# Hybrid decoder layer on one core: first projections between the last x tiles, first weight tile earlier in the load queue

## The reference, cut to what matters

```python
h = concat([meta (16 tokens), x (1024 tokens)])           # (1040, 1024), float32
u = rmsnorm(h, norm_w)
proj = u @ w_in                                           # w_in: (1024, 4104)
hg_q, hg_f, hg_i, hg_z, gd_qkv, gd_z, gd_a, gd_b = split(proj)
# HGRN2, 4 heads: gated linear attention in chunks, gated rmsnorm
# Gated DeltaNet, 4 heads: causal conv of width 4 + silu on q, k, v; g and beta from gd_a, gd_b
#   (8 columns of w_in: the gate); triangular solve per chunk; gated rmsnorm
h = h + concat(y_hg, y_gd) @ w_out
out = rmsnorm(h, final_norm_w)[16:]
```

## Time and profile before

| what | us |
|---|---|
| time, median of 3 runs (784.63 to 786.99) | 785.84 |
| the profiled execution | 786.99 |
| span in its profile | 785.3 |
| TensorE matmul busy | 725.2 (92% of the span) |
| TensorE weight loads busy (beside matmuls) | 688.1 |
| VectorE busy | 450.0 |
| GpSimd busy | 343.1 |
| ScalarE busy | 305.3 |
| the front: last matmul starts | 88.38 |
| first matmul of the next block | 90.22 |

### The profile page before, as it was taken

How to read it: one execution, slowest core, us unless ns; L and a number is a source line. 1 busy time by engine, 2 the same in 40 slices (tenths; PEclk the granted TensorE clock), 3 DMA queues, 4 the chain that set the end, 5 groups by cost and what they waited for, 6 DMA issues and landing times. The chain is left out here.

```text
span 785.3 us, 13610 instructions
## 1 busy us (share of the span) xinstructions
PE 725.2 (92%) x4852; PEld 688.1 (88%) x4852; DVE 450.0 (57%) x1011; ACT 305.3 (39%) x782; POOL 343.1 (44%) x449
## 2 busy tenths in 40 slices
PE   7799999999999999899999999999999859999975
PEld 7599999989998999899999999999899848888764
DVE  6645354378882552888824528987244266765255
ACT  6435422624543235335442263354422332132133
POOL 5573342166552421665533216754333056654124
PEclk9899999999999999999999999999999968999998
DMA  8246225030213263805355403022243042211015
GB/s 252 23 55 85 28 32 86 19 51 5 41 42 51 35 80 24 51 6 36 49 34 65 77 11 55 1 42 56 39 115 83 3 156 97 94 48 48 1 34 207
DMA packets 77030, 45.52 MB, mean 58 GB/s; under 512 B 30894, under 2 KB 72212, under 8 KB 76964
## 3 DMA queue, kind: packets, MB, share of 16 engines
q1 hardware_dynamic: 76964, 44.66, 32.4%
HBM read 36.41 MB, written 8.24 MB: 57 GB/s over the span
## 5 line engine op out<-in xcount | busy, mean ns | idle before, releaser
L221 PE MATMUL proj<-uTh,w_high 128*128 128x352 f32 (+1 forms) x768 | 262.1, 341 | 4.8 <-PEq L168 4.8
L221 PE MATMUL proj<-uTh,w_low 128*128 128x352 f32 (+1 forms) x768 | 246.3, 321 | 0.0
L221 PE MATMUL proj<-uTl,w_high 128*128 128x352 f32 (+1 forms) x768 | 245.9, 320 | 0.0
L221 PEld LDWEIGHTS proj<-uTh,w_high 128*128 128x128 f32 x768 | 145.1, 189 | 5.8 <-issue 5.7
L221 PEld LDWEIGHTS proj<-uTl,w_high 128*128 128x128 f32 x768 | 145.0, 189 | 0.0
L221 PEld LDWEIGHTS proj<-uTh,w_low 128*128 128x128 f32 x768 | 144.3, 188 | 0.0
L239 POOL TENSOR_TENSOR w_low<-w_raw,w_high 128x256 fp32r<-128x256 f32 (+1 forms) x54 | 71.0, 1314 | 95.5 <-ACT w_high L231 40.7
L1508 PE MATMUL mix<-level_x 128*128 128x128 f32 x448 | 67.0, 284 | 9.8 <-issue 4.4
L1508 PEld LDWEIGHTS mix<-level_x 128*128 128x128 f32 x448 | 62.2, 197 | 14.6 <-issue 13.2
L1150 POOL TENSOR_TENSOR f_suffix<-f_suffix,f_prefix 128x192 f32<-128x192 f32 x84 | 56.2, 669 | 22.1 <-DVE f_prefix L1337 14.1
L1347 DVE COPY_PREDICATED hg_scores<-mask_st,mix 128x384 f32<-128x384 uint8 (+1 forms) x96 | 52.1, 542 | 18.7 <-PE mix L1508 18.1
(11 more groups left out here) (309 smaller groups left out, 1381.8 us busy)
## 6 DMA issues: line engine op xcount, KB each, us to landing
w_raw<-in_w_in SPq DMA_DIRECT2D x32, 512.0 KB, 8.3
x_tile<-in_x SPq DMA_DIRECT2D x8, 512.0 KB, 7.4
w_raw<-y_scratch SPq DMA_DIRECT2D x8, 384.0 KB, 4.5
decay<-gamma_scratch SPq DMA_DIRECT2D x4, 576.0 KB, 4.1
landing<-in_w_out SPq DMA_DIRECT2D x4, 512.0 KB, 7.6
landing<-in_x SPq DMA_DIRECT2D x3, 512.0 KB, 3.6
y_scratch<-gd_y SPq DMA_DIRECT2D x6, 192.0 KB, 1.8
decay<-in_w_out SPq DMA_DIRECT2D x2, 512.0 KB, 4.0
```

The source lines that it names most:

```text
L221: last = pe.matmul(acc[:, 0:tw], w[j % 2][:, k, :], u[:, k, t0:t0 + tw], start=(k == 0 and i == 0), stop=(k == KT - 1 and i == 2))
```

## The change

On PE the gate pieces move behind the transposes of all tiles. 3 parts of the projection are put behind tile 6, 3 behind tile 7 and 10 behind tile 8: together the first two pieces. Then come the three gate pieces, the third piece, and the small gate transposes; what follows them moves back by two pieces each. On SP weight tile 0 and the two parameter broadcasts stand ahead of x tile 5 instead of behind x tile 8. ACT rounds weight tile 0 behind tile 4, POOL makes its low part there. The diagonal matrices are made from the identity in SBUF; its copy in PSUM and the semaphore for it are gone. Two memsets and one select of POOL move behind its tile loop. The number of tiles that ACT and POOL work ahead goes from 4 to 3, with the step written ahead of the tile's own work instead of behind it.

```diff
-    ident_ps = bank[5][:, 384:384 + P]
-    AHEAD = 4
+    BESIDE = {6: range(0, 3), 7: range(3, 6), 8: range(6, 2 * PARTS)}
+    AHEAD = 3
...
@@ sync
-            for i in range(2, XS):
+            for i in range(2, 5):
+                load_x(i)
+            load_tile(0, tile_cols("gd", GD_KINDS[0], 0))
+            sp.dma_start(pr[:, 0, :], A_log[0:1, :].broadcast_to([P, HEADS])).then_inc(prm_in, 16)
+            sp.dma_start(pr[:, 1, :], dt_bias[0:1, :].broadcast_to([P, HEADS])).then_inc(prm_in, 16)
+            for i in range(5, XS):
                 load_x(i)
             sp.dma_start(gate_raw[:, :, :], w_in_v[:, :, AB_COLS:AB_COLS + 2 * HEADS]).then_inc(gate_in, 16)
             for i in range(XS, NC):
                 full(sp, front, ("x", i - XS, 1))
                 load_x(i)
-            load_tile(0, tile_cols("gd", GD_KINDS[0], 0))
-            sp.dma_start(pr[:, 0, :], ...)
-            sp.dma_start(pr[:, 1, :], ...)
@@ gpsimd
             for i in range(NC):
-                low_part(pool, 2 * i + 1)
                 if i + AHEAD < NC:
                     rstd_tile(i + AHEAD)
-            early_low(0)
+                low_part(pool, 2 * i + 1)
+                if i == 4:
+                    early_low(0)
@@ scalar
             for i in range(NC):
+                if i + AHEAD < NC:
+                    square_tile(i + AHEAD)
...
                 for half in range(2):
                     high_part(2 * i + half)
-                if i + AHEAD < NC:
-                    square_tile(i + AHEAD)
-                if i == 5:
+                if i == 4:
+                    early_high(0)
+                if i == 6:
                     act.wait_ge(gate_in, 16)
                     act.copy(gate_h, gate_raw[:, :, :]).then_inc(gate_high, 1)
+                    act.wait_ge(prm_in, 32)
+                    act.activation(ea[:, :], pr[:, 0, :], ACT.Exp).then_inc(gate_exp, 1)
-            early_high(0)
-            take_gate(0)
...
+            take_gd_front(act, 0, split=False)
             early_high(1)
-            take_gd_front(act, 0, split=False)
+            take_gd_front(act, 1, split=False)
+            for g in range(len(PIECES)):
+                take_gate(g)
+            take_gd_front(act, 2, split=False)
+            early_high(2)
+            first_tap(0)
@@ vector
-                dve.tensor_scalar(diag[i % DIAGS][0:w, 0:w], ident_ps[0:w, 0:w], rstd[0:w, i:i + 1], None,
+                dve.tensor_scalar(diag[i % DIAGS][0:w, 0:w], ident[0:w, 0:w], rstd[0:w, i:i + 1], None,
                                   ALU.mult).then_inc(scaled, 1)
...
-                if n == 13:
+                if n == 14:
                     dve.wait_ge(gate_high, 1)
...
+            conv_taps(1)
             for g in range(NG):
                 decay_diff(dve, 0, g, dec_in, dec_sub)
-            conv_taps(1)
@@ tensor
-            pe.transpose(ident_ps, ident[:, :], ident[:, :]).then_inc(ident_there, 1)
...
-                if i == 6:
-                    gate_piece(0)
-            gate_piece(1)
-            gate_piece(2)
-            project(range(0, PARTS))
+                project(BESIDE.get(i, ()))
+            for g, (t0, tw) in enumerate(PIECES):
+                ...                                   # the body of gate_piece(g)
+            project(range(2 * PARTS, 3 * PARTS))
             pe.wait_ge(gate_out, len(PIECES))
...
-            project(range(PARTS, 3 * PARTS))
+            project(range(3 * PARTS, 5 * PARTS))
```

More of the change, by code:

```diff
@@ L415, in _ @@
             pool.tensor_copy(mask_st[:, 0, :], ident[:, :]).then_inc(consts, 1)
[L416 to L421, removed]
             def early_low(n):
@@ L550, in _ @@
             act.activation(gw[:, 5, :, :], gw[:, 3, :, :], ACT.Ln, bias=1.0).then_inc(gate_exp, 1)
[L551 to L554, removed]
             take_gd_front(act, 3, split=False)
+            take_gd_front(act, 4, split=False)
             act.wait_ge(gate_step, 12)
@@ L633, in _ @@
             last.then_inc(mask_set, 1)
-            dve.wait_ge(ident_there, 1)
-            for i in range(DIAGS - 1):
+            dve.wait_ge(const0, 4)
+            for i in range(AHEAD - 1):
                 diag_tile(i)
@@ L644, in _ @@
             for n in range(2 * NC):
-                if n % 2 == 0 and n // 2 + DIAGS - 1 < NC:
-                    diag_tile(n // 2 + DIAGS - 1)
+                if n % 2 == 0 and n // 2 + AHEAD - 1 < NC:
+                    diag_tile(n // 2 + AHEAD - 1)
                 norm_part(n)
@@ L728, in project @@
                     project_part(pe, n, 1)
[L730 to L738, removed]
-                        last = pe.matmul(gbank[g % 2][0:4 * HEADS, 0:tw], gate_w[:, k, :], u[:, k, t0:t0 + tw],
-                                         start=(k == 0 and n == 0), stop=(k == KT - 1 and n == 1))
-                last.then_inc(gate_done, 1)
+            pe.wait_ge(rows_in, 80)
             pe.wait_ge(const0, 4)
-            pe.transpose(ident_ps, ident[:, :], ident[:, :]).then_inc(ident_there, 1)
-            pe.wait_ge(rows_in, 80)
             ap, done = take(pe, front, "rows")
@@ L757, in _ @@
                     last.then_inc(done, 1)
-                if i == 6:
-                    gate_piece(0)
-            gate_piece(1)
-            gate_piece(2)
-            project(range(0, PARTS))
+                project(BESIDE.get(i, ()))
+            for g, (t0, tw) in enumerate(PIECES):
+                for low in u_low:
+                    pe.wait_ge(low, 1 + -(-(t0 + tw - META) // P))
+                pe.wait_ge(gate_low, 1)
+                if g >= 2:
+                    pe.wait_ge(gate_out, g - 1)
+                for k in range(KT):
+                    for n, u in enumerate((uh, ul)):
+                        last = pe.matmul(gbank[g % 2][0:4 * HEADS, 0:tw], gate_w[:, k, :], u[:, k, t0:t0 + tw],
+                                         start=(k == 0 and n == 0), stop=(k == KT - 1 and n == 1))
+                last.then_inc(gate_done, 1)
+            project(range(2 * PARTS, 3 * PARTS))
             pe.wait_ge(gate_out, len(PIECES))
@@ L778, in _ @@
             pe.matmul(ap[:, 0:HEADS * NC], ones[:, :], g_all, start=True, stop=True).then_inc(done, 1)
-            project(range(3 * PARTS, 3 * PARTS + 3))
+            project(range(5 * PARTS, 5 * PARTS + 3))
             pe.wait_ge(gate_step, 10)
@@ L782, in _ @@
             pe.transpose(ap[0:HEADS * NC, 0:P], gam[:, :, :].rearrange("p h c -> p (h c)"), ident[:, :]).then_inc(done, 1)
-            project(range(3 * PARTS + 3, 4 * len(PIECES) * PARTS))
+            project(range(5 * PARTS + 3, 4 * len(PIECES) * PARTS))
     end_block()
```

14 lines of the change are left out of this document (6 added, 8 removed).

## The result

| kernel | median us | kernel before, same chip | ratio, 95% interval |
|---|---|---|---|
| changed | 790.81 (788.96 to 792.2, 6 runs) | 786.13 (782.72 to 787.77, 6 runs) | 1.0064 [1.0039, 1.0089] |
| changed, second series | 789.91 | 787.03 | 1.0023 [1.0007, 1.0039] |
| changed, third series | 790.74 | 787.19 | 1.0047 [1.003, 1.0064] |

The changed kernel is slower: by 5.0, 1.8 and 3.7 us, if each ratio is taken times 787. All three intervals lie above 1. I had forecast 786.1 with a range that ended at 789.9; the median is above it. The profiled execution took 788.67 us with a span of 786.9. The profiled execution of the second series was disturbed; its profile is not read and its time is left out.

What follows compares the result with a forecast made beforehand. PE, busy 92% of the span, was taken to bound the kernel. Restart +0.5 us, gap -0.3 and clock 0 summed to +0.2, giving 786.1 us against the median, with a range of 782.7 to 789.9.

Steps and rivals of the forecast that it cites:

- How the front adds up: Front's end is PE's restart after its last long pause, plus the dense work behind it, plus the clock loss.
- the gap of 0.29: PE's one idle gap after its restart, at 38.88; the gate pieces no longer meet it: -0.3 us.
- the clock's 2.2: Clock falls in PE's pause and stays at half speed 4.3 us after restart, losing 2.2 us, same as before: 0.
- The set of work behind the restart, and the new wait: PE has the same work left after its restart; its wait for the gate becomes one for weight tile 0's low part.
- The landing of tile 5: The weight tile ahead in the queue delays x tile 5 by 4.1 us, to 16.8, between 15.2 and 18.5.
- The chain from tile 5 to `w_low`: ACT and POOL work from tile 5's landing to the weight's low part takes 11.5 us, ending at 28.3.
- L: Time at which x tile 5 lands and its square can start; forecast 16.8, from 15.2 to 18.5.
- port: Rival: DVE's diagonals from SBUF wait for POOL's low parts; +1.3 us for one on the path, +2.4 for two; chance 0.15.
- warm: Rival: PE's clock does not fall in the pause or recovers sooner; -2.0 us, -3.6 with early landing; chance 0.24.
- held: The forecast case: PE's wait for the gate becomes a wait for w_low of like length; +0.2 us; chance 0.47.
- Long half speed: Rival: PE stays slow 9.2 us after its restart, not 4.3, losing another 2.4 us; +2.6 us; chance 0.14.
- The sum: Front's end: restart 28.3 instead of 27.76, +0.5; gap -0.3; clock 0; total +0.2 us, from -1.4 to +1.9.

Runs made afterwards that it cites:

- e2: The changed kernel with the diagonals made from the identity in PSUM again; 788.22 us, ratio 1.0020 to the kernel before.
- e7: The changed kernel with the two parameter broadcasts behind x tile 8 again, weight tile 0 still ahead of tile 5; 790.58 us, ratio 1.0047 to the kernel before.
- e9: The changed kernel itself, measured again as the third series; 790.74 us, ratio 1.0047 to the kernel before.
- e4: The changed kernel with SP's old load order and the identity in PSUM, PE's new order kept; 784.25 us, ratio 0.9964 to the kernel before.
- e3: The changed kernel with weight tile 0 and the two broadcasts behind x tile 8, as before; 785.5 us, ratio 0.9977 to the kernel before.
- e5: The kernel before with only the diagonals' identity taken from SBUF; 790.7 us, ratio 1.0047 to the kernel before.
- e6: The kernel before with only SP's order changed, weight tile 0 and both broadcasts ahead of x tile 5; 791.08 us, ratio 1.0061 to the kernel before.
- e8: e4 with projection piece 0 cut: high-part matmuls behind tile 6, low-part ones behind tile 7, second piece behind tile 8; 779.83 us, ratio 0.9921 to the kernel before.
- e10: The changed kernel with only projection piece 0 cut by operand, early weight tile and SBUF identity kept; 788.2 us, ratio 1.0012 to the kernel before.
- e1: The changed kernel itself, measured again as the second series; 789.91 us, ratio 1.0023 to the kernel before.

## Why the prediction was wrong, step by step

**How the front adds up: right, and better than I knew.** Take the front's end less the restart. The changed kernel has 58.47 us, e2 58.48, e7 58.47. Before it is 60.93; less the gap of 0.29 and the clock's 2.2 that is 58.4. e9 has 60.03, e4 59.75, e3 60.10; each of these showed a clock near one half at or soon after the restart. So the dense work is 58.4 to 58.5 us in all, and only two terms vary: the restart, and 0 to 1.6 us of clock. With PE's old order the same sum, less the gap of 0.3, leaves 3.0 us of clock in e5 and 1.8 in e6. The clock's share is a remainder, but it fits the rows: e9 did 16 matmuls where the first profile did 29, which is 1.7 us of full speed.

**The set of work behind the restart, and the new wait: right.** The wait for the gate became a wait for `w_low`, released by POOL, as said. It is 1.72 us and not 2.8, since a part of the stall had moved ahead of tile 5's transposes.

**The landing of tile 5: the step that failed.** I took the weight tile's service as 4.1 us, the middle of 2.5 and 5.6, and so 16.8 for the landing, 18.5 at most. Measured were 18.63, 19.08, 19.41 and more: against the 12.7 of the kernel before, the weight tile in front cost tile 5 5.9 us in the first profile, 6.4 and 6.7 in e9 and e2, and not 4.1. The lower bound should have had no weight: the 2.5 us between the landings of tile 8 and weight tile 0 were what was left over: the weight tile had been issued at 11.47, and part of it was served beside x tiles. The 5.6 us between two weight tiles was the price of one, and the row of GB/s in 17.60:23.00, 76 against 374, would have said so. I had read the DMA share, which is as high in both, as the measure of the queue. For the changed kernel's first profile the error is 1.8 us; with e9 and e2, 2.3 and 2.6 us.

**The chain from tile 5 to `w_low`: right in its parts, one port short.** I had L + 11.5. Without the port it is 11.05 (e2) and 11.90 (e4); with it 12.56, 12.54 (e9), 12.55 (e7) and 12.33 (e3). The rival "port", at 0.15, came true: the diagonals of tiles 5, 6 and 7 took 1.30 to 1.40 us. On the path that is 1.0 us against the forecast chain and 1.5 against e2, where tile 5 is late too; with tile 5 on time it is 0.4 (e3 against e4). Two diagonals had been priced at +2.4. Why only a part of their waits reaches the path is not tried. My argument against it was that POOL waits for ACT ahead of most low parts. It does. But ACT's second half releases POOL some 0.6 us after its first has released DVE's low part, which takes 0.69 us; so DVE comes to the diagonal as POOL starts, and in the changed kernel the two meet at each of these tiles. This is read from the rows, not tried by itself. The Trainium skill (SBUF - State Buffer, Who interferes with whom) has the rule that who comes second waits for the whole instruction; 0.28 against 1.21 and 1.22 us in e5, beside a low part of 1.27, agrees with it.

**The clock: right on what happens in a pause, wrong on where.** I had the loss as before, 2.2 us, and one pause. There were two, and it fell in the first. Its half speed then fell on the transposes of tiles 5 and 6, where PE had to wait anyway. At the restart the loss was 0 (the first profile, e2, e7) or 1.6 (e9). That is the rival "warm" in one execution and "held" in another of the same kernel. "Long half speed" did not come in the changed kernel; in e5 the half speed lasted somewhat longer than before, 5.7 us instead of 4.3. Its argument stays unexplained: the 43 matmuls in 5.40:15.00 came at a granted clock of 1.00, so the row doesn't show half speed.

**The sum, with what was measured.** Restart 31.19 - 27.76 = +3.43, gap -0.29, clock -2.2: +0.94, where +0.97 is seen. With e9: 31.62 - 27.76 = +3.86, -0.29, -0.6: +2.97, where +2.96 is seen. I had +0.5, -0.3 and 0. The restart is 2.9 us later than forecast, 1.8 of it the landing and 1.0 the ports. The landing is a mis-sized term; the ports were a rival that the sum left out. That the first profile's front still ends only 0.8 us behind the forecast 88.9 is luck: the clock's 2.2 us came back in just that execution. The range had slips too. Late L with long half speed is +1.9 + 2.4 = +4.3 and not +4.1, and warm with an early L is -3.6 and not -3.2, which gives 782.2 to 790.1; the median lies above that as well.

**What stays open.** The times of the changed kernel stand 1.8 to 5.0 us above the kernel before, the fronts of the two good profiles 1.0 and 3.0. With e2 to e8 and e10 the time follows the front within 0.4 us (e3, e4, e8, e10) to 1.8 us (e5). Where it is over half a microsecond, the surplus is on the slow side. It also decides the range: the fronts alone, +1.0 and +3.0 on 785.84, would have stayed inside it (786.8 and 788.8).

A profile is one execution, and not always a typical one: the first profile's, 788.67 us, is faster than all six timed ones of its series, and e9's, 793.84, is slower than all but one of its ten. What lies behind the front is the same code in all kernels, and yet it is not equally long. Span less front is 696.6 us before, 697.2 in the changed kernel's first profile, 700.4 in e9, 701.2 in e6 and 694.4 in e8. The starts of the blocks show where e9 lost against the first profile. The third block behind the front took 68.9 us before and in the first profile (248.33 to 317.26) and 71.4 in e9 (250.36 to 321.74). Its first 10 us, in e9 and then in the first profile:

```profile
250.36:260.36 10.00, 10.00 (x60) 9.92 (x61) 1.55 (x5) 4.67 (x19) 3.87 (x6) 0.83 0.49 72
248.33:258.33 10.00, 9.99 (x72) 9.92 (x73) 2.52 (x9) 5.12 (x19) 4.93 (x7) 1.00 0.50 72
```

The clock fell there in e9, and just so in e3 (60 matmuls at 0.83), which has the old load order. The fifth block took 69.0 us in the first profile, 69.6 before, 71.0 in e9 and 72.7 in e6; PE waits there for DVE (`gd_n`) for 1.78 us in e9 and 1.93 in e6, and not at all in the first profile. So a part of the surplus is clock and waits in unchanged code, which differ from one execution of a kernel to the next. Whether the change makes them more frequent, by where it leaves the later loads or in some other way, no run here tells, and so the rest of the medians' difference stays open.

**What the parts are worth.** By differences of ratios: PE's order -0.36% (e4), the cut of piece 0 another -0.43% (e8 less e4, on two chips), SP's order +0.46% (e1 to e3) or +0.61% (e6), the identity +0.13% (e3 to e4; their intervals overlap) or, in the kernel before, +0.47% (e5). These are differences of single measurements with intervals of 0.2 to 0.3% to each side, so those that lie close are not told apart.

## What to carry to other kernels

Before a load is moved ahead of others in a full queue, read the GB/s of the stretch in which it is served, not the busy share: the price of being in front goes by its size over its own rate, and who is behind it may be more urgent. Here 512 KB at 111 and 76 GB/s are 4.7 and 6.9 us, and tile 5 was 5.9 to 7.8 us late. When two engines are released by the same third one, their instructions start together; an operand that moves from PSUM to SBUF can then meet the other engine's instruction each time, and a scaling of 0.35 us takes 1.3. Where a matmul group waits for one of its operands only, start it with the parts that need the others: that gained 0.35 to 0.43% here, about as much as PE's new order (0.36%).

## What the hardware showed that I had not expected

- Weight tiles (512 KB) came at 76 to 111 GB/s, x tiles of the same size at 374, the DMA share being 0.94 to 1.05 in all three windows. In 5.40:15.00 the DMA view has 1087 of 1927 packets under 512 B and nearly all others over 2 KB before, and 942 of 1546 between 512 B and 2 KB in the changed kernel; it moved 2.11 MB instead of 3.36. Whether the packets' size is what makes the weight tile slow is not tried:

```profile
DMA packets 1546, 2.11 MB, mean 220 GB/s; under 512 B 207, under 2 KB 1149, under 8 KB 1546
```

- An x tile behind a weight tile took 11.5 us (changed kernel) and 15.2 us (e7) from issue to landing, without it 7.9. SP's issue of tile 8 lasted 8.69 us in e7, and 3.32 in the changed kernel.
- A scaling of 128 x 128 f32 by DVE: 0.35 us from PSUM, 0.28 from SBUF where it got in ahead of POOL, 1.21 to 1.40 from SBUF where it waited for a POOL low part.
- The clock can fall behind a restart: in e3 it read 1.00 in 26.80:28.30, PE being busy all of it after a pause of 2.89 us, and then 0.50:

```profile
26.80:28.30 1.50, 1.50 (x9) 1.50 (x10) 0.66 (x2) 0.00 (x0) 1.42 (x3) 1.00 0.18 30
28.30:31.60 3.30, 3.30 (x19) 3.30 (x17) 3.21 (x5) 1.47 (x4) 1.29 (x2) 0.50 1.02 64
```
